# Three thirds of the tokens side by side in the feed-forward blocks of a hybrid decoder step

## The reference

```
def finish(x, m, w_o, g_post_mix, g_pre_ffn, g_post_ffn, w_gate, w_up, w_down):
    x = x + rmsnorm(m @ w_o, g_post_mix)
    h = rmsnorm(x, g_pre_ffn)
    f = (silu(h @ w_gate) * (h @ w_up)) @ w_down      # 1024 -> 2816 -> 1024
    return x + rmsnorm(f, g_post_ffn)
```

## Time and profile before

| | us |
|---|---|
| median of three runs | 3122.59 |
| the profiled execution | 3121.17 |
| its span, first to last instruction | 3119.4 |
| busy in it: TensorE matmul | 3018.1 (97%) |
| weight load | 2641.5 (85%) |
| VectorE / ScalarE / GpSimd | 1405.3 / 1054.1 / 735.6 |

### The profile page before, as it was taken

How to read it: one execution, slowest core, us unless ns; L and a number is a source line. 1 busy time by engine, 2 the same in 40 slices (tenths; PEclk the granted TensorE clock), 3 DMA queues, 4 the chain that set the end, 5 groups by cost and what they waited for, 6 DMA issues and landing times. The chain is left out here.

```text
span 3119.4 us, 48922 instructions
## 1 busy us (share of the span) xinstructions
PE 3018.1 (97%) x19766; PEld 2641.5 (85%) x19766; DVE 1405.3 (45%) x3342; ACT 1054.1 (34%) x2094; POOL 735.6 (24%) x526
## 2 busy tenths in 40 slices
PE   8999999989999999999999999998899999999998
PEld 6777756569999999999977777665799999999997
DVE  5579575447621111122565887654574211111115
ACT  4366525554311111011333765354552111110112
POOL 3002031315322222243300201312252222122131
PEclk9999999999999999999999999999999999999999
DMA  5120325552211111121321112456511111111131
GB/s 176 40 63 28 105 100 187 198 173 83 82 44 48 48 48 47 42 65 58 120 75 47 48 35 90 154 187 203 173 58 60 42 47 48 48 48 41 48 117 56
DMA packets 254074, 263.55 MB, mean 84 GB/s; under 512 B 24994, under 2 KB 224571, under 8 KB 253851
## 3 DMA queue, kind: packets, MB, share of 16 engines
q1 hardware_dynamic: 233370, 189.11, 19.5%
q0 software_dynamic: 20480, 71.32, 6.7%
HBM read 229.73 MB, written 30.65 MB: 83 GB/s over the span
## 5 line engine op out<-in xcount | busy, mean ns | idle before, releaser
L2220 PE MATMUL ps<-act_lo,w_hi 128*128 128x352 f32 x2112 | 683.5, 324 | 5.6 <-DVE act_lo L2672 3.9
L2220 PE MATMUL ps<-act_hi,w_hi 128*128 128x352 f32 x2112 | 677.0, 321 | 0.0
L2220 PE MATMUL ps<-act_hi,w_lo 128*128 128x352 f32 x2112 | 676.7, 320 | 0.0
L2594 POOL TENSOR_TENSOR w_lo<-w_raw,w_hi 128x1024 fp32r<-128x1024 f32 x132 | 323.1, 2450 | 1022.0 <-ACT w_hi L2434 1022.0
L725 PE MATMUL ps<-w_in_slots,hT 128*128 128x256 f32 (+1 forms) x2048 | 448.2, 375 | 3.4 <-PEq L193 3.4
L725 PEld LDWEIGHTS ps<-w_in_slots,hT 128*128 128x128 f32 x2048 | 373.9, 192 | 59.4 <-issue 12.8
L2220 PEld LDWEIGHTS ps<-act_lo,w_hi 128*128 128x128 f32 x2112 | 396.2, 188 | 11.3 <-DVE act_lo L2672 5.9
L2220 PEld LDWEIGHTS ps<-act_hi,w_hi 128*128 128x128 f32 x2112 | 396.9, 188 | 0.2
L2220 PEld LDWEIGHTS ps<-act_hi,w_lo 128*128 128x128 f32 x2112 | 395.9, 187 | 0.0
L2685 DVE TENSOR_TENSOR a_raw<-ps,silu 128x352 f32<-128x352 f32 x120 | 62.9, 524 | 728.7 <-PE ps L2220 721.7
L2220 PE MATMUL ps<-a_lo,w_hi 128*128 128x352 f32 x1056 | 344.0, 326 | 0.0
(11 more groups left out here) (369 smaller groups left out, 4250.5 us busy)
## 6 DMA issues: line engine op xcount, KB each, us to landing
w_raw<-in_w_gate SPq DMA_DIRECT2D x44, 512.0 KB
w_raw<-in_w_up SPq DMA_DIRECT2D x44, 512.0 KB, 5.2
w_raw<-in_w_down SPq DMA_DIRECT2D x44, 512.0 KB, 5.4
w_in_slots<-in_w_in SPq DMA_DIRECT2D x18, 1024.0 KB, 5.3
xpark<-xT SPq DMA_DIRECT2D x9, 1408.0 KB, 5.7
xT<-xpark SPq DMA_DIRECT2D x6, 1408.0 KB, 15.8
hT<-xpark SPq DMA_DIRECT2D x6, 1408.0 KB
wo_raw<-in_w_o SPq DMA_DIRECT2D x16, 512.0 KB, 5.0
```

The costliest lines, as they stand in the source:

```text
L2220: ins = pe.matmul(bank(b), w, x, start=first and i == 0, stop=end and i == 2)
L2594: pool.tensor_tensor(w_lo[slot(j)][:, 0:K, :], w_raw[slot(j)][:, 0:K, :], w_hi[slot(j)][:, 0:K, :].bitcast(F32), ALU.subtract).then_inc(w_ ...
```

## The change

For the 56 blocks behind the first four, the three units of a block are no longer worked one after the other. TensorE waits for all three banks and for `w_lo` at the start of the block. Then, for each k and for each of the three terms, it issues three matmuls with the same weight operand, one for each third, into three banks. The three accumulations of a block end in three successive matmuls, each of which raises `mm` by one. In the first down block of a part, the wait at each k is for the last third's `a_lo`. The first four blocks, the down projection behind all blocks, and the lists of the other engines are as they were, and so is the number of matmuls.

```
-            for n, (j, th) in enumerate(seq):
+            n_pre = n_of[NPRE, 0]
+            for n, (j, th) in enumerate(seq[:n_pre]):
+                wait_bank(n)
...
+            for n in range(n_pre, len(seq), 3):
+                j = seq[n][0]
+                what, p_, i, _ = blocks[j]
+                K = sources[j].shape[1]
+                for th in range(3):
+                    wait_bank(n + th)
+                pe.wait_ge(w_lo_done, j + 1)
+                for k in range(K):
+                    if what == "down" and i == 0:
+                        pe.wait_ge(a_lo_done, up_nth[chunk(p_, k), 2])
+                    x_hi, x_lo = (a_hi[k], a_lo[k]) if what == "down" else (act_hi[:, k, :], act_lo[:, k, :])
+                    hi, lo = w_hi[slot(j)][:, k, :], w_lo[slot(j)][:, k, :]
+                    for i_term, (w, x) in enumerate(((hi, x_lo), (hi, x_hi), (lo, x_hi))):
+                        for th in range(3):
+                            ins = pe.matmul(bank(unit_bank(n + th)), w, x[:, of(th)], start=k == 0 and i_term == 0, stop=k == K - 1 and i_term == 2)
+                            if k == K - 1 and i_term == 2:
+                                ins.then_inc(mm, 1)
```

More of the change, by code:

```diff
@@ L2273, in _, with wait_bank @@
                         mix_sum_2(0)
-            for n, (j, th) in enumerate(seq):
-                what, p_, i, _ = blocks[j]
-                K = sources[j].shape[1]
+            def wait_bank(n):
                 user = bank_user(n)
@@ L2287, in _ @@
                     pe.wait_ge({"gate": sg_done, "up": mul, "down": dn}[kind(user)], nth[user])
+            n_pre = n_of[NPRE, 0]
+            for n, (j, th) in enumerate(seq[:n_pre]):
+                wait_bank(n)
                 if th == 0:
                     pe.wait_ge(w_lo_done, j + 1)
-                for k in range(K):
+                for k in range(KC):
                     if j == 0:
                         pe.wait_ge(h_lo, KC * th + k + 1)
[L2293 to L2296, removed]
+                    ins = terms(unit_bank(n), w_hi[slot(j)][:, k, :], w_lo[slot(j)][:, k, :], act_hi[:, k, of(th)], act_lo[:, k, of(th)], k == 0, k == KC - 1)
                 ins.then_inc(mm, 1)
```

## The result

The changed kernel takes 3146.0 us (median of six runs, 3140.82 to 3149.97), the kernel before 3122.88 us in the same set of runs (3119.96 to 3123.24): a ratio of 1.0074, 95% interval 1.0063 to 1.0084. It is slower by 23 us; the profiled execution, 3145.57 us, by 24.4.

A forecast was written before the change was run, and what follows sets the result against it. The prediction took each matmul's own weight load on TensorE as the bound, not the 352 columns. Terms of 0, 0 and 3.7 us (layer ends) on 3122.59 gave 3126.3 us, range 3117 to 3138.

The forecast's parts named there:

- No load is dropped, repeated weights save nothing: In the rewritten blocks, 9 loads for 9 matmuls remain although three successive matmuls share weights: term 0.
- The rival that reuse works: In the rewritten blocks, repeated weight loads cost nothing, saving 75 us: 3051 us, chance 0.07.
- The load binds, not the 352 columns: In the feed-forward blocks, each matmul waits for its own 188 ns weight load, setting the 159 ns distance.
- Another bank at each matmul, and another third: no change: In the rewritten blocks, same operands equally often keep the matmul distance: term 0, bounds -8 to +15 us.
- The cadence rival: Gate and up units slow to 160.0 ns, 3132.1 us, or all to 161.1, 3141; chance 0.35.
- Waits at the start of a block: Four waits in a row at each rewritten block's start, hidden behind TensorE's own 11.45 us per block: term 0.
- The end of the blocks, 1.85 us a layer: Behind each layer's last up block, the down projection waits for VectorE to read three banks: 3.7 us in all.
- The clock: Rival: TensorE stands or turns through banks and the granted clock falls to 0.50: 3131 us, chance 0.03.

The follow-up runs named there:

- the grouped order: Changed kernel with thirds 0 and 2 first in each k (but a block's last), all three terms, then third 1: 3097.47 us, 1.0023 of the kernel before.

## Why the prediction was wrong

*No load is dropped, repeated weights save nothing.* Right, and now tried: with the new weight order alone the stretch is the same to 0.02 us. The rival that reuse works, 3051 us, is out.

*The load binds, not the 352 columns.* Wrong. I took it from one width: a load that starts with the matmul before it and the next matmul 0.16 us later looks the same when the load only follows the stream. The distance falls with the columns down to 256, at 0.42 ns each. The Trainium skill ("TensorE: Matmul & The Clock Gate", section on LDWEIGHTS) has P/1.2 ns for a load of P columns, so 107 for 128; the floor of 111 ns at 192 and 128 columns lies 4 ns above it, and I should have wondered at a load that binds at 159. The sum didn't rest on this step, but the next did in part: with the load as the bound, the moving operand's order seemed idle.

*Another bank at each matmul, and another third: no change.* This term failed; it was 0 and measured 19.9 us, 2.47 ns for each of 8064 matmuls. The bank has no part in it. The moving operand has, and my argument for it was additive: the same operands equally often, so the same mean. The same operands, equally often, cost 2.9 ns more each in gate and up blocks and 1.6 ns more in down blocks once their order was new: a distance depends on the sequence and on the place against the weights. The rows had a hint: the same shape ran at 158.3, 160.0 and 161.1, and I said that I couldn't derive these levels. In hindsight the tile of k = 1, at 158.3, lies at the odd place and that of k = 2 at the even one. That their mean came near the level of gate and up units says nothing of another order, and I took it for an argument. As bounds the levels were right only in part: the upper end was 161.1, and the measured mean lies above it. The cadence rival had the direction, and its price at 161.1, 3141, was 5 us short.

*Waits at the start of a block.* Right: TensorE has no gap in either stretch.

*The end of the blocks, 1.85 us a layer.* Right, 1.86 us, with its times; and removed by the last block in the old order.

*The clock.* It stayed at 1.00 in the stretch and at the waits. The Trainium skill ("TensorE: Matmul & The Clock Gate", "A second HAM failure mode: psum-queue depth-cycling") tells of a clock that swings in a kernel that cycles through banks, where TensorE idles shortly between groups of matmuls. I cited it without that idling. Here three banks turned without any idle time and the clock stayed at 1.00 over 652 us.

*The range.* It ended at 3138, since I gave 161.1 throughout as the far end and left it out. A level that I couldn't derive deserved a range that reached beyond the levels seen, and 3146 would have asked for 161.7 throughout.

**What stays open.** Why the distance depends on the places in this way. The runs exclude the banks, the repeats of a weight operand and 64-byte lines as such (32 bytes on everything changed nothing), and show a period of 128 bytes for the two orders and more than one level for one sequence. They don't give a law from which the table could be worked out. The sequences under 159.0 (all starts odd, 158.3; 0 and 32 bytes in turn, 156.7) were not tried in a complete kernel: they need each tile padded, by my count 4 KB and more in a memory that these buffers fill. Complete, 158.3 would be worth about 8 us, an estimate from 0.7 ns x 5760 and 1.7 ns x 2304; whether down blocks get there no run shows. No kernel that ran beats the one before.

## What to carry to other kernels

Matmuls in succession on the same weights gained nothing here, where each came with its own load; look at the two counts first. Where a stream of matmuls fills the time, their distance is to be read to a tenth of a nanosecond, and any new order or new buffer address is a change of it by up to some per cent, in either direction. Before one reorders such a loop, a probe with another sequence in each block tells in one run roughly what each would cost. Give each sequence two blocks at least and read the later one: one sequence read 8 ns apart in two places, and the grouped order came 0.5 ns dearer than I had judged. And three accumulations that end together hand their readers a queue: that is hidden inside a loop and bare at its end.

## What the runs showed of the hardware that I had not expected

- A matmul of 128x128 by N columns in fp32r, with its own load, comes every N x 0.417 ns and some 13 ns at clock 1.00 (146.7 at 320, 119.9 at 256; 2 ns less than that at 304), and 111 ns at 192 and at 128.
- Its distance depends on where the moving operand starts against the weights, in steps of 4 bytes: 159.0 to 164.4 ns for the old order over all places tried (164.4 at 72 bytes), 159.6 to 165.2 for the new.
- The same sequence ran at 158.3 ns in one block and at 166.7 in another.
- With the old order, moving all buffers by 32 bytes leaves the stretch as it is (642.21 us), and moving the activations alone costs 2.9 us a stretch (645.17 and 645.12).
